# A two-block network on one core: low-rank products, key norms and decays of the recurrent layer placed under its projections, attention logits from 64 rows, another order at the entrance

## What is computed

```python
def dsa_mixer(h, w_in, w_o):
    q, k, v, qi, ki, wi = split(h @ w_in)          # 16 heads of 64, 4 key heads, 8 index heads of 64
    q, k, qi, ki = rope(q), rope(k), rope(qi), rope(ki)
    rel = relu(einsum('bthd,bsd->bths', qi, ki))
    score = einsum('bths,bth->bts', rel, wi)       # causal, then the 64 largest of a row
    p = softmax(einsum(q, k_selected) * 64 ** -0.5)
    return (p @ v_selected) @ w_o

def rwkv7_mixer(h, mu, w_rkv, w0, w1, w2, a0, a1, a2, g1, g2, k_k, k_a, r_k, lnx_w, lnx_b, w_o):
    xx = token_shift(h) - h
    xs = h[None] + xx[None] * mu[:, None, None, :]            # six mixes
    r, k, v = einsum('cbld,cde->cble', xs[:3], w_rkv)         # three 1024x1024 projections
    xw, xa, xg = xs[3], xs[4], xs[5]
    w_log = -softplus(-(w0 + tanh(xw @ w1) @ w2)) - 0.5       # w1: 1024x64, w2: 64x1024
    decay = exp(-exp(w_log))
    a = sigmoid(a0 + (xa @ a1) @ a2)
    g = sigmoid(xg @ g1) @ g2                                 # g1: 1024x160
    kk = normalised over each head of 64 (k * k_k)
    k = k * (1 + (a - 1) * k_a);  b = kk * a
    # per step: S = S*w + (S @ -kk) b^T + v k^T;  y = S r
    return ((norm(y) + bonus) * g) @ w_o
```

## Time and profile before

| | us |
|---|---|
| median of three runs | 1157.73 |
| profiled execution | 1157.85 |
| its span, first to last instruction | 1155.9 |
| mean granted TensorE clock | 0.973 of full |

### The profile page before, as it was taken

The page is one execution under the profiler, slowest core; times in us unless marked ns, Lnnn a source line. Parts: engine busy times, 40 slices in busy tenths (PEclk is TensorE's granted clock), DMA queues, the critical chain, the costliest instruction groups (busy, mean ns, idle before and its releaser), DMA issues.

```text
span 1155.9 us, 23371 instructions
## 1 busy us (share of the span) xinstructions
PE 1091.5 (94%) x9368; PEld 985.6 (85%) x9368; DVE 811.1 (70%) x1071; ACT 630.3 (55%) x917; POOL 227.4 (20%) x171
## 2 busy tenths in 40 slices
PE   6898999999989998999699999989999999999987
PEld 5786798899879876999489989969998899998785
DVE  4687457767769759775765776787757777785574
ACT  4666356565556457323347556654444566665552
POOL 1000033345510003944103533540000000000000
PEclk9998999999999997999799999999999999999999
DMA  7522287877735520000258787756665455656400
GB/s 276 187 74 74 73 265 253 282 255 250 253 119 177 186 80 2 4 3 3 85 195 269 252 262 260 258 164 196 184 186 182 146 183 180 200 166 211 150 1 37
DMA packets 82137, 190.33 MB, mean 165 GB/s; under 512 B 5840, under 2 KB 6112, under 8 KB 81936
## 3 DMA queue, kind: packets, MB, share of 16 engines
q1 hardware_dynamic: 73184, 157.31, 41.6%
q0 software_dynamic: 7584, 27.53, 8.2%
q10 hardware_dynamic: 1296, 4.44, 1.0%
HBM read 188.21 MB, written 1.05 MB: 164 GB/s over the span
## 4 chain that ended last, share of the span: by engine, by line
PE 74%; DVE 11%; ACT 4%; issue 4%; DMA 4%; POOL 2%; DVEq 0%; ACTq 0%; POOLq 0%; SPq 0%
PE bank L1952 12%; PE bank L1954 12%; PE bank L1953 12%; PE bank L1928 4%; PE bank L1929 4%; PE bank L1930 4%; PE bank L2347 4%; PE bank L2171 4%; PE bank L2173 3%; PE bank L2172 3%; DVE w_lo L1195 3%; DMA mod_w<-in_w_mod_dram 2%; POOL mod_all L523 1%; PE bank L2243 1%; PE bank L2459 1%
## 5 line engine op out<-in xcount | busy, mean ns | idle before, releaser
L1195 DVE TENSOR_TENSOR w_lo<-raw,w_hi 128x1024 fp32r<-128x1024 f32 x296 | 390.7, 1339 | 208.1 <-ACT w_hi L665 207.8
L665 ACT ACTIVATE w_hi<-raw 128x1024 fp32r<-128x1024 f32 x296 | 309.5, 1056 | 294.2 <-PE bank L1954 148.3
L1952 PE MATMUL bank<-act_hi,w_hi 128*128 128x256 f32 x1392 | 390.0, 280 | 1.4 <-DVE act_lo L1237 0.8
L1954 PE MATMUL bank<-act_hi,w_lo 128*128 128x256 f32 x1392 | 389.0, 279 | 0.0
L1953 PE MATMUL bank<-act_lo,w_hi 128*128 128x256 f32 x1392 | 388.3, 279 | 0.0
L1952 PEld LDWEIGHTS bank<-act_hi,w_hi 128*128 128x128 f32 x1392 | 261.6, 188 | 4.2 <-issue 2.8
L1953 PEld LDWEIGHTS bank<-act_lo,w_hi 128*128 128x128 f32 x1392 | 261.6, 188 | 0.9 <-issue 0.2
L1954 PEld LDWEIGHTS bank<-act_hi,w_lo 128*128 128x128 f32 x1392 | 261.5, 188 | 0.0
L523 POOL TENSOR_TENSOR mod_all<-mod_all,mod_w 128x1024 f32<-128x1024 f32 x42 | 110.0, 2620 | 141.6 <-ACT mod_w L842 140.7
L2171 PE MATMUL bank<-w_hi,ff_hi 128*128 128x512 f32 x256 | 102.3, 400 | 7.4 <-DVE ff_lo L1434 7.4
L2173 PE MATMUL bank<-w_hi,ff_lo 128*128 128x512 f32 x256 | 101.7, 397 | 0.0
(11 more groups left out here) (311 smaller groups left out, 1440.0 us busy)
## 6 DMA issues: line engine op xcount, KB each, us to landing
raw<-in_mlp_w_up_dram SPq DMA_DIRECT2D x64, 512.0 KB, 4.9
raw<-in_mlp_w_down_dram SPq DMA_DIRECT2D x64, 512.0 KB, 4.5
raw<-in_dil_w_in_dram SPq DMA_DIRECT2D x64, 512.0 KB, 4.1
mod_w<-in_w_mod_dram POOLq DMA_DIRECT2D x48, 512.0 KB, 4.4
raw<-in_conv_w_in_dram SPq DMA_DIRECT2D x32, 512.0 KB, 4.4
raw<-in_rwkv_w_rkv_dram SPq DMA_DIRECT2D x24, 512.0 KB, 4.6
raw<-in_dsa_w_in_dram SPq DMA_DIRECT2D x16, 512.0 KB, 5.2
raw<-in_dsa_w_o_dram SPq DMA_DIRECT2D x8, 512.0 KB, 3.7
```

What stands on the lines that cost most here:

```text
L665: act.activation(w_hi[:, slot, :], raw[:, slot, :], ACT.Copy).then_inc(hi_ready, 1)
L1195: dve.tensor_tensor(w_lo[:, slot, :], raw[:, slot, :], w_hi[:, slot, :].bitcast(F32), ALU.subtract).then_inc(lo_ready, 1)
L1952: pe.matmul(dst, w_hi[:, slot, at], hi[:, kt, :], start=begin, stop=False, skip_group_check=True)
L1954: mm = pe.matmul(dst, w_lo[:, slot, at], hi[:, kt, :], start=False, stop=end, skip_group_check=True)
```

## The change

1. The mixes get tiles of their own: `MIXED = (act_f, f_w, f_a, rr, act_f, act_f)`, with `f_w` and `f_a` over `uv` and the third over `rr`. Their order becomes k, decay, rate, r, v, gate; the projections run in the order k, r, v (`KINDS`).
2. TensorE computes the decay's and the rate's low-rank products together after block 1, alternating between column halves of the array and writing the two halves of the rows of one bank. After block 3 come the gate's product, the head sums and half of the second low-rank products; after two granules of block 4 the spread; after block 4 the other half.
3. ScalarE and VectorE do the gates, key norms, decays and `early_operands` of both units in `rwkv_in`, between the splits of the granules; one mean reduction moves into the scan.
4. After block 5 remain: the gate's output, now in banks 0 to 3, behind the copies of the values; ScalarE's `decays(1)` and the four gate copies. The first unit waits for these, and the values are turned after it, before the second unit, in banks 4 to 7.
5. GpSimd loads `g2` after the gate's product and waits for `operands` of both units before its own share.
6. Attention: no zero fills and no `kiT`; index logits and logits multiply 64 rows at a time, the two halves alternating into two banks. The order of heads in the score sum and of the maxima follows. ScalarE rectifies the first four index logits before it copies the keys.
7. Entrance: the first rounding of the activations goes between the second and third granule's; the larger part of the constants, the final scale and the gate biases are loaded on ScalarE's queue after the queries' third copy (`late_loads`); the first MLP waits for the constants.

```diff
+                def lora_decay_and_rate():
+                    pe.wait_ge(mod_ready, 4)
+                    pe.wait_ge(mixed, 12)
+                    for kt in range(KT):
+                        for m, rows in enumerate((slice(0, LORA), slice(LORA, P))):
+                            mm = pe.matmul(bank[4][rows, 0:SEQ], R[("w1", "a1")[m]][:, kt, :], MIXED[1 + m][:, kt, :],
                                            start=kt == 0, stop=kt == KT - 1)
                     mm.then_inc(lora_full, 1)
...
+                        if n == 4 and q == 1:
+                            pe.wait_ge(rw_inverse, 1)
+                            pe.wait_ge(lora2_ready, 4)
+                            spread(4).then_inc(kk_spread, 1)
+                    if n == 1:
+                        lora_decay_and_rate()
                     if n == 3:
-                        lora(0, ((0, LORA),))
+                        lora_gate()
+                        pe.wait_ge(kk_squared, 1)
+                        head_sums(1, R["kk_square"]).then_inc(kk_sums, 1)
+                        second_lora(0)
                     if n == 4:
-                        lora(1, ((0, LORA),))
-                lora(2, ((0, GHALF), (GHALF, GHALF)))
+                        pe.wait_ge(kk_ready, 4)
+                        second_lora(1)
```

ScalarE's new order from block 3 on, and VectorE's from the key product on:

```diff
+                splits(18, 20)
+                leave(3)
+                act.wait_ge(lora_full, 2)
+                act.activation(R["gmid"][:, :, :], bank[0][0:GHALF, :].rearrange("p (m t) -> p m t", m=2), ACT.Sigmoid).then_inc(mid_ready, 1)
+                root(1)
+                open_gates(0)
                 keep_a(0)
+                splits(20, 21)
                 decays(0)
+                splits(21, 24)
+                leave(4)
+                open_gates(1)
                 keep_a(1)
+                leave(5)
+                decays(1)
...
+                dve.tensor_tensor(R["raw_kk"], R["k"][:, :, :], K_K.unsqueeze(2).broadcast_to([P, PAIRS, SEQ]), ALU.mult).then_inc(kk_made, 1)
+                splits(14, 15)
                 dve.wait_ge(mix_lo, 12)
+                mix_part(5, 0, 1)
+                splits(15, 16)
+                mix_part(5, 2, 3)
+                splits(16, 20)
+                dve.wait_ge(kk_sums, 1)
+                dve.tensor_scalar(per_head[:, :], bank[1][:, 0:SEQ], 1e-24, None, ALU.max).then_inc(sums_ready, 1)
+                invert(1)
+                sum_decays(0)
+                splits(20, 21)
+                for b in range(4):
+                    final_kk(b)
...
+                splits(21, 22)
...
+                splits(22, 24)
...
+                early_operands(0)
+                dve.wait_ge(lora2_full, 8)
+                sum_decays(1)
+                early_operands(1)
+                means(0)
```

The scan's entrance, and the logits:

```diff
                         if it == 0:
                             pe.wait_ge(operands, u + 1)
-                            pe.wait_ge(*((vT_ready, 4) if u == 0 else (glora_ready, 4)))
+                            if u:
+                                turn_values()
+                            pe.wait_ge(*((glora_ready, 4) if u == 0 else (vT_ready, 4)))
...
                     for j in range(2):
-                        dst = bank[2 * slot + j][:, 0:2 * w].rearrange("p (e s) -> p e s", e=2)
-                        pe.matmul(dst, ident_bf, S["bias"][:, i:i + 1, 0:w].broadcast_to([P, 2, w]), start=True, stop=False, skip_group_check=True)
-                        mm = pe.matmul(dst, S["qT"][:, 2 * n + j, i * P:(i + 1) * P], S["kT"][:, n, :, 0:w],
-                                       start=False, stop=True, skip_group_check=True)
+                        for e in range(2):
+                            rows = slice(e * HD, (e + 1) * HD)
+                            mm = pe.matmul(bank[2 * slot + e][:, j * w:(j + 1) * w], S["qT"][rows, 2 * n + j, i * P:(i + 1) * P],
+                                           S["kT"][rows, n, 0:w], start=False, stop=True, skip_group_check=True)
```

More of the change, by code:

```diff
@@ L911, in rwkv_in, with splits, keep_a @@
                     round_mix(0, (b,))
-                split_block(base, 4)
-                round_mix(1)
+                def splits(first, last):
+                    for k in range(first, last):
+                        split_hi(base, k)
+                def keep_a(half):
+                    act.wait_ge(less_ready, 1)
+                    act.wait_ge(kk_sums, 1)
+                    act.wait_ge(lora2_ready, 4 * half + 4)
+                    for pair in range(4 * half, 4 * half + 4):
+                        kept = act.activation(R["ka"][:, pair, :], mixer["a"][:, pair, :], ACT.Identity, bias=less_k_a[:, pair:pair + 1], scale=K_A[:, pair:pair + 1])
+                    kept.then_inc(ka_ready, 1)
@@ new lines, in open_gates @@
+                def open_gates(half):
+                    for pair in range(4 * half, 4 * half + 4):
+                        act.wait_ge(lora2_full, 2 * (pair // 2) + 2)
+                        src = slice(pair % 2 * SEQ, (pair % 2 + 1) * SEQ)
+                        for j, (bias, dst) in enumerate(((W0, less), (A0, mixer["a"]))):
+                            sg = act.activation(dst[:, pair, :], bank[4 + 2 * (pair % 4 // 2) + j][:, src], ACT.Sigmoid, bias=bias[:, pair:pair + 1])
+                        sg.then_inc(lora2_ready, 1)
@@ new lines, in rest_part, with splits @@
+                def rest_part(j, *parts):
+                    for b in parts:
+                        dve.wait_ge(mix_hi, 4 * j + b + 1)
+                        at = (slice(None), slice(2 * b, 2 * b + 2), slice(None))
+                        dve.tensor_tensor(act_lo[j % 2][at], MIXED[TO_SPLIT[j]][at], act_hi[j % 2][at].bitcast(F32), ALU.subtract).then_inc(mix_lo, 1)
+                def splits(first, last):
+                    for k in range(first, last):
+                        split_lo(base, k)
@@ new lines, in sum_decays @@
+                def sum_decays(half):
+                    at = slice(4 * half, 4 * half + 4)
+                    for pair in range(4 * half, 4 * half + 4):
+                        dve.wait_ge(lora2_ready, pair + 1)
+                        sc = dve.tensor_tensor_scan(R["cum"][:, pair, :], view["keep"], less[:, pair, :], 0.0, ALU.mult, ALU.add)
+                    sc.then_inc(cum_ready, 1)
+                    dve.wait_ge(cum_ready, half + 1)
+                    dve.tensor_tensor(less[:, at, :], R["cum"][:, at, :], less[:, at, :], ALU.subtract).then_inc(cum_less, 1)
@@ L1566, in rwkv_in @@
[L1566 to L1580 removed]
+                gate_rows(0, (4, 5))
@@ new lines, in second_lora @@
+                def second_lora(half):
+                    if half == 0:
+                        pe.wait_ge(mid_ready, 2)
+                    else:
+                        pe.wait_ge(lora2_ready, 4)
+                    for pair in range(4 * half, 4 * half + 4):
+                        for j, rows in enumerate((slice(0, LORA), slice(LORA, P))):
+                            mm = pe.matmul(bank[4 + 2 * (pair % 4 // 2) + j][:, pair % 2 * SEQ:(pair % 2 + 1) * SEQ], R["w2a2"][rows, pair * P:(pair + 1) * P],
+                                           R["mid"][rows, :], start=True, stop=True)
+                        mm.then_inc(lora2_full, 1)
```

394 lines of the change are left out of this document (188 added, 206 removed).

## The result

| | before | after |
|---|---|---|
| median | 1160.61 (17 runs, 1153.70 to 1165.36) | 1152.17 (17 runs, 1144.87 to 1155.93) |
| profiled execution, its span | 1157.85, 1155.9 | 1153.22, 1151.5 |
| its mean granted clock | 0.973 | 0.970 |

The ratio of the runs is 0.9924, 95% interval 0.9905 to 0.9942: 8.8 us faster, where the forecast had 14.2. A second comparison of the same two kernels, with 6 and 17 runs, gave 0.9897 (0.9872 to 0.9922), 12.0 us. The forecast of 1143.6, with a range up to 1151.0, was too fast.

A forecast was written before the change was run, and what follows sets the result against it. TensorE was taken to bound the projections and the scan from the second unit's first product, which VectorE's last operand releases. 1157.85 less 11.0 (recurrent layer) and 3.2 (attention) gave 1143.6 us, range 1137.5 to 1151.

The forecast's parts named there:

- The recurrent layer was to give 11.0: Recurrent layer: second unit 13.4 earlier, less 0.4 for the mean reduction and 2.0 for the clock.
- Attention was to give 3.2: Attention: 1.2 from an earlier first unit and 2.0 over the last units; bounds 0.5 and 5.
- The clock behind the gap ahead of the first unit: Recurrent layer: TensorE's clock falls at a gap of about 2.5 until the values are turned, costing 2.0.
- The mean reduction moved into the scan: Scan: it stands on VectorE ahead of the first square's transpose, charged 0.4, bounds 0 and 2.6.
- attention's units: Attention: halved logits save at most about 1.0 a unit, which may come down to 3.9; 2.0 over the last units.
- changes between 128-row and 64-row products: Attention's units: a change of tiling mode was said to drain TensorE; no drain was seen, so nothing was charged.
- the likeliest case: Whole kernel: as summed, 1142.5 to 1147, the upper end with the clock lost within the gate output; chance 0.38.
- (e): Recurrent layer: a late copy or operand holds the second unit near where it was, 1152 to 1163; chance 0.06.
- (f): Projections: VectorE's split becomes the bound and the kernel is slower, 1168 if 20 granules wait 1.2 each; chance 0.04.
- (a): Recurrent layer: the clock stays up, 13.0 in place of 11.0, 1141.6, down to 1138 with attention's whole 5; chance 0.30.
- (c): Small stalls: granules wait for splits or column halves don't overlap (3.5), attention gives 0.5; 1147 to 1151.5; chance 0.16.
- The MLP between is unchanged.: MLP between attention and recurrent layer: unchanged, its wait for the moved constants coming 70 us after their issue.

The follow-up runs named there:

- the part alone: Kernel before with only the recurrent layer's hunks: ratio 0.9938; or with only 64-row logits, split constant loads and entrance order: 0.9987.
- The experiment with the values first: Changed kernel with the values turned right behind the gate output, ahead of the first unit: median 1148.82, ratio 0.9894 against the kernel before.
- the earlier splits: Kernel before with attention's part of the change and VectorE's splits of attention's last four granules one place earlier: 1155.73, ratio 0.9971.

## Why the prediction missed

The order of events in the recurrent layer was forecast rightly, and both terms of the sum came out smaller. The recurrent layer was to give 11.0; its stage gave 8.9, and the part alone gave 7.2 in the runs (4.5 to 10.0). Attention was to give 3.2; the part alone gave 1.5 (between 4.2 faster and 1.3 slower). Three steps failed. The clock behind the gap ahead of the first unit was charged 2.0 and took 2.7. The mean reduction moved into the scan was charged 0.4 and took 1.8. And attention's units were to come down to 3.9 each and came to 4.30, since changes between 128-row and 64-row products, put at nothing, cost TensorE 0.4 in each. A fourth term was missing altogether: what a lower clock over attention's units takes back, by the fit the largest in attention (3.9).

**Right, step by step.** The projections took 85.6 (85.4 forecast) with no granule waiting for its split; VectorE was busy 75.2 of 85.6 (78 of 88). Decay and rate took 3.67 (3.6), gate 7.07 (7.1), head sums 1.07 (1.0), second products 4.00 in two groups (3.7 in one), spread 1.15 (1.3). The gate output took 7.10 (7.0 to 7.3) and released nothing; the first unit started at 95.7 (95.2), released by ScalarE's gate copies. The clock fell at the gap ahead of it, as the likeliest case had it. Rivals (e) and (f) are out, and (a) as well. The time lies just above the range of (c), but its mechanism, granules that wait or column halves that don't overlap, is out too; only its small gain in attention came.

**The clock's price in the first unit.** This term was undersized. The sum charged 0.8 on the first unit and some 1.2 on the values. The unit's two groups took 3.9 instead of 2.2, 1.7 more, and the values 4.82 instead of 3.8, 1.0 more. With a start 0.5 later the second unit was 3.2 late against 101.8, where 2.0 were charged. The experiment with the values first shows the cause: without the gap the groups and the values are at their full-clock times.

**The mean reduction.** It was charged at 0.4 with bounds 0 and 2.6; the two waits are 1.21, the turn is 1.8 longer, and with the reduction ahead of the scan the 1.8 are gone. The argument was VectorE's share (26.5 busy of 39.7), and a share says nothing of a reduction that stands ahead of exactly the transpose that TensorE needs next. The clock (0.7), the late start (0.5) and the reduction (1.4) cost 2.6 more than charged; the stage lacks 2.1 of the 11.0 (8.9), so some 0.5 was won elsewhere in it.

**Attention.** The forecast was 3.2, measured are 1.5 alone and 3.4 with the earlier splits: by these intervals the size could still be right, but the steps are not those of the forecast. The first unit's maxima start 0.5 earlier (82.60 against 83.09), not 1.2: the last granule ended at 81.47 and not at 80.3 to 81.1, as the clock fell in the gap of 3.55. The units take 4.30 and not 3.9, and what binds them is TensorE, which has no gap between these rows. First the kernel before, then the changed one:

```profile
111.51 0.38 PE L2109 MATMUL bank<-sel_bias,const_bf 128*128 128x512 bf16 x1
111.72 1.02 PE L2110 MATMUL bank<-kT,qT 128*128 128x512 f32 x2
112.58 0.38 PE L2109 MATMUL bank<-sel_bias,const_bf 128*128 128x512 bf16 x1
112.80 1.02 PE L2110 MATMUL bank<-kT,qT 128*128 128x512 f32 x2
113.65 1.90 PE L2136 MATMUL bank<-v,probsT 128*128 128x64 f32 x16
115.39 1.04 PE L2122 MATMUL bank<-const,probs 128*128 128x128 f32 x8
```

```profile
109.49 1.04 PE L2177 MATMUL bank<-const,probs 128*128 128x128 f32 x8
110.37 0.59 PE L2161 MATMUL bank<-sel_bias,const_bf 128*128 128x512 bf16 x2
110.89 1.13 PE L2165 MATMUL bank<-kT,qT 64*128 64x256 f32 x8
111.96 2.00 PE L2191 MATMUL bank<-v,probsT 128*128 128x64 f32 x16
113.79 1.05 PE L2177 MATMUL bank<-const,probs 128*128 128x128 f32 x8
```

From start to start a unit took 4.77 (110.62 to 115.39) and takes 4.30 (109.49 to 113.79). The two logits took 1.72 and half of that is 0.86, which would make the unit 3.9, just the forecast. They take 1.07 (110.89 to 111.96), and the bias and the values have each grown by 0.09. The missing 0.4 stands at the two places where TensorE goes from 128-row to 64-row products and back. These rows are of narrow windows of the same timeline, the second of the bias and the second and third pair of logits:

```profile
110.58 0.38 PE L2161 MATMUL bank<-sel_bias,const_bf 128*128 128x512 bf16 x1
111.21 0.38 PE L2165 MATMUL bank<-kT,qT 64*128 64x256 f32 x2
111.43 0.38 PE L2165 MATMUL bank<-kT,qT 64*128 64x256 f32 x2
```

A step between starts is 0.21 to 0.22 here. It is 0.31 into the first pair (110.58 to 110.89), 0.32 into the second, 0.22 into the third, and again 0.32 from the fourth pair into the values (111.64 to 111.96); the step behind that one has grown by 0.1 too. The prediction had this cost before it and read it as nothing, for it compared an end with a start (430.52 and 430.45). Products overlap in these rows, each lasts 0.38 at a step of 0.21, so an end behind the next start proves nothing. By starts the change shows there as well: 0.33 (430.12 to 430.45), where the groups of head sums before it follow at 0.22. So a unit saves 0.47 and not the 0.87 of the forecast. What TensorE does in that time the trace does not show.

Even so, the fit gives the part 4.7 at equal clock, more than the 3.2. That most of it does not arrive is put down to the clock over the units, whose price was charged in the recurrent layer and forgotten here. This is read from traces and a fit; no experiment removed it.

**"The MLP between is unchanged."** Its work is; what it waits for is not always the same. Its modulation loads are issued when attention's output is done, and their arrival, through ScalarE's queue, can hold the first down product. In both traces of the changed kernel TensorE waited 3.0 and 3.3 there instead of 1.4, and lost 1.5 more by the clock behind it; behind the waits of 1.97 and 1.99 in two other kernels the clock stayed at 1.00. The same wait was between none and 2.0 in seven other kernels with this order, and taking it away moved no median. So it is a part of the scatter, and it is not shown to be one of the shortfall.

**The base and the range.** The sum stood on one execution, 1157.85. The kernel before then had medians of 1160.61, 1160.83, 1159.92 and 1158.29, and single runs from 1153.5 to 1167.3. With 14.2 taken from 1160.6 it would have been 1146.4. The range held the cases of the change and no term for that scatter, though the three runs shown (1156.93 to 1162.38) had a spread of 5.5 us. Of the 8.6 us between forecast and median, 2.8 are the base (1160.61 less 1157.85) and 5.8 the gain. Of the 5.8 the stage has 2.1 and attention 1.7 by its own runs; some 2 are in no stage, and a second comparison with a gain of 12.0 instead of 8.8 says that so much is scatter.

## What to carry to other kernels

When the engine that sets the time gets a pause, price the clock behind it on everything until it recovers, and see whether some ready work of the same engine fits into the pause: moving 128 small products into a gap of 3.1 us brought the second unit 6.9 us forward. A moved instruction of 2.5 us is free only if the next one in its queue is not awaited; check that neighbour, not the engine's share. Read whether products follow each other closely from their starts, since their ends overlap. And where single runs of one kernel scatter by 1%, take the base from many of them, and read stages from traces and totals from runs.

## What was not expected of the hardware

- A row of VectorE with 128x16 values took 2.20 us beside a GpSimd row with two inputs of 2.36 (437.72 to 440.08) and ended 0.03 behind it. It took 0.17 to 0.18 with no GpSimd row beside it, and 0.23 beside one with a single tensor as input. A row 32 times as large (128x512) took 2.60 to 2.74 beside such rows and 0.67 without, so it is the GpSimd row that sets the time:

```profile
437.91 2.20 DVE L1657 TENSOR_SCALAR v_mean<-v_mean 128x16 f32<-128x16 f32 x1
```

- A change between products of 128 and of 64 rows cost TensorE some 0.1 us at the change and 0.1 more at the next step, 0.4 in each attention unit of 4.30.
- Products in alternating halves of the columns ran side by side (16 in 3.67), the same in two runs of eight did not (6.32).
- The length of a gap alone does not say whether the clock falls. Behind 2.19 (in the kernel before), 2.92, 3.01 and 3.13 it fell to 0.50, behind 1.97, 1.99 and 2.10 it did not. But behind the same gap of 3.67 ahead of the old index logits the clock was 0.58 in the kernel before (54.2 to 58.2) and 1.00 in the recurrent part alone (54.5 to 58.5).
- A pause taken from TensorE at one place of attention (3.55 to 1.61) came back at the next as a wait of 2.42, and the clock with it: 0.89 and 0.65 over two windows became 1.00 and 0.53.
